# A decoder block on one core: VectorE instead of GpSimd makes the second MLP matrix's low halves, both token halves are streamed as one operand, and bias rows and sums of squares are rounded

## The reference, cut to what matters

```
h = rmsnorm(x, norm_attn);  proj = h @ w_in            # 512 tokens x 1024
o_nsa = nsa_attention(...)                             # T5 relative bias by distance
o_sb  = stick_breaking_attention(...)
mixed = sigmoid(..) * (o_nsa @ w_up_nsa) + sigmoid(..) * (o_sb @ w_up_sb)
x = x + mixed @ w_out
h = rmsnorm(x, norm_mlp)
x = x + square(relu(h @ w_ff1)) @ w_ff2                # 1024 -> 4096 -> 1024
return rmsnorm(x, norm_final)
```

## Time and profile before

| | |
|---|---|
| runs, us | 784.09, 781.94, 784.12 (median 784.09) |
| profiled execution, its own time | 782.67 us |
| its span from first to last instruction | 780.8 us |
| mean granted TensorE clock | 0.995 |
| busy share | PE 99%, PEld 83%, DVE 59%, ACT 50%, POOL 36% |

### The profile page before, as it was taken

How to read it: one execution, slowest core, us unless ns; L and a number is a source line. 1 busy time by engine, 2 the same in 40 slices (tenths; PEclk the granted TensorE clock), 3 DMA queues, 4 the chain that set the end, 5 groups by cost and what they waited for, 6 DMA issues and landing times.

```text
span 780.8 us, 11862 instructions
## 1 busy us (share of the span) xinstructions
PE 770.2 (99%) x4292; PEld 650.1 (83%) x4292; DVE 461.1 (59%) x936; ACT 387.9 (50%) x719; POOL 277.5 (36%) x366
## 2 busy tenths in 40 slices
PE   8999999999999999999999999999999999999996
PEld 6878888888877777778888888999999999999895
DVE  7446557787757676635544737556665556664334
ACT  6333314688966576574345644344444444443321
POOL 1255424511112332146455644333333322233640
PEclk9999999999999999999999999999999999999998
DMA  7954013210150110134232223332222333332213
GB/s 261 340 180 163 1 55 101 88 54 29 35 155 28 55 55 29 55 108 148 95 108 98 91 101 115 109 108 88 85 93 88 108 109 109 108 108 81 87 49 109
DMA packets 26006, 77.82 MB, mean 100 GB/s; under 512 B 3710, under 2 KB 6966, under 8 KB 25695
## 3 DMA queue, kind: packets, MB, share of 16 engines
q1 hardware_dynamic: 23868, 74.72, 29.0%
q10 hardware_dynamic: 2083, 2.37, 1.0%
HBM read 73.90 MB, written 2.13 MB: 97 GB/s over the span
## 4 chain that ended last, share of the span: by engine, by line
PE 93%; DVE 4%; ACT 2%; DMA 1%; issue 1%; DVEq 0%; ACTq 0%
PE bank L1508 31%; PE bank L1914 20%; PE bank L1888 5%; PE bank L1886 5%; PE bank L1884 5%; PE bank L1820 2%; PE bank L1802 2%; PE bank L1734 2%; PE bank L1859 2%; PE bank L1858 2%; PE bank L1854 2%; PE bank L1779 2%; PE bank L1752 1%; PE bank L1520 1%; PE bank L1521 1%; PE bank L1522 1%
## 5 line engine op out<-in xcount | busy, mean ns | idle before, releaser
L644 POOL TENSOR_TENSOR wlo<-wraw,whi 128x256 fp32r<-128x256 f32 x344 | 262.8, 796 | 461.4 <-ACT whi L685 378.6
L685 ACT ACTIVATE whi<-wraw 128x1024 fp32r<-128x1024 f32 x77 | 80.6, 1053 | 32.0 <-PE bank L1914 19.1
L1508 PE MATMUL bank<-hh,wlo 128*128 128x512 f32 x304 | 81.0, 396 | 0.7 <-DVE gm L1202 0.6
L1508 PE MATMUL bank<-hl,whi 128*128 128x512 f32 x304 | 80.6, 392 | 0.0
L1508 PE MATMUL bank<-hh,whi 128*128 128x512 f32 x304 | 79.6, 391 | 0.0
L1508 PEld LDWEIGHTS bank<-hh,whi 128*128 128x128 f32 x304 | 56.6, 188 | 11.7
L1508 PEld LDWEIGHTS bank<-hl,whi 128*128 128x128 f32 x304 | 56.4, 188 | 11.7 <-issue 0.2
L1508 PEld LDWEIGHTS bank<-hh,wlo 128*128 128x128 f32 x304 | 55.4, 188 | 12.8 <-DVE gm L1202 0.9
L1914 PE MATMUL bank<-r_l,whi 128*128 128x512 f32 x224 | 57.9, 390 | 0.0
L1914 PE MATMUL bank<-r_h,wlo 128*128 128x512 f32 x224 | 56.3, 392 | 0.0
L1914 PE MATMUL bank<-r_h,whi 128*128 128x512 f32 x224 | 55.7, 389 | 0.0
(11 more groups left out here) (310 smaller groups left out, 1647.1 us busy)
## 6 DMA issues: line engine op xcount, KB each, us to landing
wraw<-in_panels SPq DMA_DIRECT2D x101, 512.0 KB, 3.3
land<-in_panels SPq DMA_DIRECT2D x12, 512.0 KB, 4.5
w1k<-in_w SPq DMA_DIRECT2D x1, 2048.0 KB, 9.3
w1v<-in_w SPq DMA_DIRECT2D x1, 2048.0 KB, 14.8
svraw<-in_panels SPq DMA_DIRECT2D x4, 512.0 KB, 5.3
hank<-bias_by_distance SPq DMA_DIRECT2D x4, 512.0 KB, 6.3
x_res<-in_xT SPq DMA_DIRECT2D x4, 512.0 KB, 4.4
out_dram<-x_res SPq DMA_DIRECT2D x12, 128.0 KB, 1.8
```

What stands on the lines that cost most here:

```text
L644: ins = nc.gpsimd.tensor_tensor(wlo[:, s, k:k + 2], wraw[s][:, k:k + 2], whi[:, s, k:k + 2].bitcast(F32), ALU.subtract)
L685: A(whi[:, s], wraw[s][:], ACT.Copy).then_inc(w_hi, 1)
L1508: ins = M(b[:, cols], lhs, (xl if a == 1 else xh)[:, row + k, cols], start=(m == 0), stop=(m == 23))
```

## The change

1. `products` takes the input's high and low halves as one operand of two runs of 256 columns. For each of four weight tiles there is one matmul of 512 columns, high weights by (high, low), whose two results lie beside each other in a bank, and one of 256 columns, low weights by high input. That makes 8 matmuls in place of 12. `h2h` and `h2l` become halves of `h2`, `th` and `tl` of `tt`.
2. The right half of each bank now holds a part of the sum, so it is added by VectorE: two adds more in `c11`, one each in `c22`, `c12` and `c21`, and two new steps `m7_low` and `u2`. `c12` now starts with a ScalarE copy. TensorE waits for `u2_made` (VectorE) instead of `u2_copied` (ScalarE).
3. In the rounds, VectorE makes the low halves of the second matrix's panels (`second_matrix_low`, one instruction of 128x1024); GpSimd makes those of the first two and the last eight.
4. The four full-precision matmuls become pairs of rounded ones: the table, the two sums of squares and the ones are rounded into `relx_r`, `oneh_r`, `sqs_r`, `x_ss_r` and `ones_r`, with the low half as a second part.

```diff
@@ gpsimd
-            for p in range(P_SQK + RING * rounds, N_PLAIN):
-                low(p)
+            for m in range(2):
+                low(P_FF2 + m)
+            pool.wait_ge(w_lo, P_FF2 + 2 * N_SEVEN)
+            for m in range(2 * N_SEVEN, 32):
+                low(P_FF2 + m)
@@ scalar
+            act.wait_ge(sqs_done, KT)
+            A(sqs_r[:, 0], sqs[:], ACT.Copy).then_inc(sqs_hi, 1)
+            act.wait_ge(table_in, 16 * 3)
+            A(oneh_r[:], oneh[:], ACT.Copy).then_inc(table_hi, 1)
...
+            act.wait_ge(x_ss, KT)
+            A(x_ss_r[:, 0], mx[0][:], ACT.Copy).then_inc(x_ss_hi, 1)
...
+            def c12_high(j):
+                A(tmp[:, 0, T // 2:T], result(act, ("wa", j))[:, 0:T // 2], ACT.Copy).then_inc(c12_copied, 1)
...
-                    stored(act, ("wa", j - 1))
+                    c12_high(j - 1)
+                    act.wait_ge(pos1, j)
                     hidden_high(8 + 2 * j - 2)
@@ vector
+            dve.wait_ge(sqs_hi, 1)
+            V.tensor_tensor(sqs_r[:, 1], sqs[:], sqs_r[:, 0].bitcast(F32), ALU.subtract).then_inc(sqs_lo, 1)
...
+            dve.wait_ge(x_ss_hi, 1)
+            V.tensor_tensor(x_ss_r[:, 1], mx[0][:], x_ss_r[:, 0].bitcast(F32), ALU.subtract).then_inc(x_ss_lo, 1)
...
+            def second_matrix_low(m):
+                dve.wait_ge(w_lo, p)
+                dve.wait_ge(w_hi, p + 1)
+                V.tensor_tensor(wlo[:, s], wraw[s][:], whi[:, s].bitcast(F32), ALU.subtract).then_inc(w_lo, 1)
...
             def c11(j):
-                V.tensor_tensor(tmp[:, 0, near], bank[j % 2][:, near], tmp[:, 0, near], ALU.add).then_inc(c11_made, 1)
+                emptied(V.tensor_tensor(t, x[:, far], t, ALU.add), ("wx", j))
+                V.tensor_tensor(t, a[:, near], t, ALU.add).then_inc(c11_made, 1)
+                V.tensor_tensor(t, a[:, far], t, ALU.add).then_inc(c11_made, 1)
...
+            def u2(j):
+                dve.wait_ge(u2_copied, j + 1)
+                V.tensor_tensor(u2s[:], bank[j % 2][:, far], u2s[:], ALU.add).then_inc(u2_made, 1)
...
                 pair_second_low(j)
+                if j:
+                    second_matrix_low(2 * j + 1)
                 c11(j)
+                m7_low(j)
...
                     first_sums(j + 1)
+                u2(j)
+                if j + 1 < N_SEVEN:
                     third_sum(j + 1)
                     pair_first_low(j + 1, 0)
+                    second_matrix_low(2 * j + 2)
@@ tensor
-                filled(M(b[0:H, :], relx[:], oneh[:, T * i:T * i + T], start=True, stop=True), f"vec{i}")
+                for part in (1, 0):
+                    ins = M(b[0:H, :], relx_r[:, part], oneh_r[:, T * i:T * i + T], start=(part == 1), stop=(part == 0))
...
                 for k in range(4):
-                    M(o, wl[:, k], xh[:, k], start=(start and k == 0), stop=False, skip_group_check=True)
+                    M(o[:], wh[:, k], x[:, :, k], start=(start and k == 0), stop=False, skip_group_check=True)
                 for k in range(4):
-                    M(o, wh[:, k], xl[:, k], start=False, stop=False, skip_group_check=True)
-                for k in range(4):
-                    ins = M(o, wh[:, k], xh[:, k], start=False, stop=(stop and k == 3), skip_group_check=True)
+                    ins = M(o[:, 0:T // 2], wl[:, k], x[:, 0, k], start=False, stop=(stop and k == 3), skip_group_check=True)
...
-                pe_.wait_ge(u2_copied, j + 1)
+                pe_.wait_ge(u2_made, j + 1)
```

More of the change, by code:

```diff
@@ L329, in block_kernel @@
         dts = place("dts", [55, H, P], at=at_sbq + 6144)
+        relx_r = place("relx_r", [BUCKETS + 1, 2, H], F32R, at=at_sbq + 14080)
+        oneh_r = place("oneh_r", [BUCKETS + 1, 2 * T], F32R, at=tmp_at)
+        sqs_r = place("sqs_r", [P, 2, T], F32R, at=at_sbq)
         relx = place("relx", [BUCKETS + 1, H], at=at_sbq + 10240)
@@ L342, in block_kernel @@
         svraw = [place(f"svraw{c}", [P, 8, P], at=at_g + 4096 * c) for c in range(RING)]
+        ones_r = place("ones_r", [P, P], F32R)
         kd1 = place("kd1", [P, 2, T], F32R, at=tmp_at)
@@ L983, in _ @@
             V.memset(relx[BUCKETS:BUCKETS + 1, :], BIG).then_inc(set_done, 1)
+            dve.wait_ge(set_done, 1)
+            V.tensor_copy(ones_r[:], ones[:]).then_inc(set_done, 1)
             for g in range(G):
@@ L1388, in pair_second_low @@
                 V.tensor_tensor(wlo[:, 3, 4:8], land[:, 4:8], whi[:, 3, 4:8].bitcast(F32), ALU.subtract).then_inc(pd_lo, 1)
+            def second_matrix_low(m):
+                p = P_FF2 + m
+                s = slot(p)
+                dve.wait_ge(w_lo, p)
+                dve.wait_ge(w_hi, p + 1)
+                V.tensor_tensor(wlo[:, s], wraw[s][:], whi[:, s].bitcast(F32), ALU.subtract).then_inc(w_lo, 1)
             def c11(j):
+                a, x, t = bank[j % 2], bank[2], tmp[:, 0, near]
+                dve.wait_ge(x_copied, j + 1)
+                emptied(V.tensor_tensor(t, x[:, far], t, ALU.add), ("wx", j))
@@ L1397, in c22, with m7_low @@
+                positive(t, t, near)
+            def m7_low(j):
+                t = tmp[:, 1, far]
+                dve.wait_ge(m7_copied, j + 1)
+                V.tensor_tensor(t, bank[3][:, far], t, ALU.add).then_inc(c22_made, 1)
+            def u2(j):
+                dve.wait_ge(u2_copied, j + 1)
+                V.tensor_tensor(u2s[:], bank[j % 2][:, far], u2s[:], ALU.add).then_inc(u2_made, 1)
             def c22(j):
+                a, t = bank[j % 2], tmp[:, 1, far]
                 dve.wait_ge(v_ready, j + 1)
-                dve.wait_ge(m7_copied, j + 1)
@@ L1401, in c22 @@
-                V.tensor_tensor(tmp[:, 1, far], bank[j % 2][:, near], tmp[:, 1, far], ALU.add).then_inc(c22_made, 1)
+                dve.wait_ge(c22_made, 3 * j + 1)
+                V.tensor_tensor(t, a[:, near], t, ALU.add).then_inc(c22_made, 1)
+                dve.wait_ge(c22_made, 3 * j + 2)
+                V.tensor_tensor(t, a[:, far], t, ALU.add).then_inc(c22_made, 1)
             def c12(j):
-                a = result(dve, ("wa", j))
-                emptied(positive(tmp[:, 0, far], a[:, near], far), ("wa", j))
@@ L1407, in c21 @@
-            def c21(j):
-                r = result(dve, ("wr", j))
-                dve.wait_ge(u2_copied, j + 1)
-                emptied(V.tensor_tensor(tmp[:, 1, near], r[:, near], u2s[:], ALU.add), ("wr", j))
+                t = tmp[:, 0, far]
+                dve.wait_ge(c12_copied, j + 1)
+                emptied(V.tensor_tensor(t, bank[j % 2][:, far], t, ALU.add), ("wa", j))
+                stored(dve, ("wa", j))
+                positive(t, t, far).then_inc(pos1, 1)
+            def c21(j):
+                r, t = result(dve, ("wr", j)), tmp[:, 1, near]
+                dve.wait_ge(u2_made, j + 1)
+                V.tensor_tensor(t, r[:, near], u2s[:], ALU.add).then_inc(c21_made, 1)
+                dve.wait_ge(c21_made, j + 1)
+                emptied(V.tensor_tensor(t, r[:, far], t, ALU.add), ("wr", j))
@@ L1612, in _ @@
             b = claim(pe_, "rms")
-            pe_.wait_ge(set_done, 4)
-            pe_.wait_ge(sqs_done, KT)
-            filled(M(b[:], ones[:], sqs[:], start=True, stop=True), "rms")
+            pe_.wait_ge(set_done, 5)
+            pe_.wait_ge(sqs_lo, 1)
+            for part in (1, 0):
+                ins = M(b[:], ones_r[:], sqs_r[:, part], start=(part == 1), stop=(part == 0))
+            filled(ins, "rms")
             bias_rows(0)
@@ L1875, in _, with products @@
             b = claim(pe_, "rms2")
-            pe_.wait_ge(x_ss, KT)
-            filled(M(b[:], ones[:], mx[0][:], start=True, stop=True), "rms2")
+            pe_.wait_ge(x_ss_lo, 1)
+            for part in (1, 0):
+                ins = M(b[:], ones_r[:], x_ss_r[:, part], start=(part == 1), stop=(part == 0))
+            filled(ins, "rms2")
             for n in range(2, 8):
                 panel(P_FF + n, ("ff", 0, n), h2h, h2l)
-            def products(o, wh, wl, xh, xl, start, stop):
+            def products(o, wh, wl, x, start, stop):
                 for k in range(4):
-                    M(o, wl[:, k], xh[:, k], start=(start and k == 0), stop=False, skip_group_check=True)
+                    M(o[:], wh[:, k], x[:, :, k], start=(start and k == 0), stop=False, skip_group_check=True)
                 for k in range(4):
-                    M(o, wh[:, k], xl[:, k], start=False, stop=False, skip_group_check=True)
-                for k in range(4):
-                    ins = M(o, wh[:, k], xh[:, k], start=False, stop=(stop and k == 3), skip_group_check=True)
+                    ins = M(o[:, 0:T // 2], wl[:, k], x[:, 0, k], start=False, stop=(stop and k == 3), skip_group_check=True)
                 return ins
@@ L1929, in _ @@
-                r = claim(pe_, ("wr", j))[:, near]
+                filled(products(x, whi[:, 2, 4:8], wlo[:, 2, 4:8], h2[:, :, 4:8, near], True, True), ("wx", j))
+                r = claim(pe_, ("wr", j))
```

(4 more changed lines are left out.)

52 lines of the change are left out of this document (31 added, 21 removed).

## The result

The changed kernel takes 777.44 us (median of five executions, 776.99 to 778.6). The kernel before takes 782.36 (median of five, 781.27 to 784.12). The ratio is 0.9933, with a 95% interval from 0.9916 to 0.995: faster by 0.7%, against about 0.3% that a measurement of this kernel can tell. The forecast was 777.2, in a range from 775.2 to 781.8.

What follows compares the result with a forecast made beforehand. The prediction took TensorE's issued matmuls to bound the kernel, since it never waits in a round. From 782.67 us it took 3.5 for joined products and 2.0 for rounded pairs, giving 777.2 us, range 775.2 to 781.8.

Steps and rivals of the forecast that it cites:

- What bounds the kernel: MLP rounds: TensorE is busy for all of 21.02 us, so what it has to issue counts.
- Part 1: Seven products a round with 8 matmuls in place of 12: 0.29 us less a round, 3.5 us in all.
- Rival 1: Joined matmuls in the products: two runs cost what two matmuls cost, 1.0 us lost, total 781.7; chance 0.12.
- the smaller saving: Joined products: with the skill's 2.5 ns fixed per matmul, only 0.8 us gained before width changes, total about 780 to 781.
- Part 2: Seven more VectorE adds a round, 2.9 us, all beside TensorE's work: 0 us; tightest room 1.5 us at `u2`.
- What a miss would cost: VectorE's adds in the rounds: once the room is gone, each microsecond late costs one a round, 12 in all.
- Part 3: Low halves of the second matrix moved to VectorE, 2.4 us a round in its idle time: 0 us.
- Part 4: Four full-precision matmuls (`rms`, two bias rows, `rms2`), 3.77 us, become rounded pairs of 1.81 us: 2.0 us gained.
- Rival 3: Near the start: the attention stage's chains set the pace, 1.4 us of gain lost, total 778.6; chance 0.08.
- The sum: Whole kernel: 782.67 of the profiled execution less 3.5 and 2.0 gives 777.2 us; from the runs' median 778.6.

Runs made afterwards that it cites:

- split kernel: The changed kernel with every 512-column matmul of the seven products cut into two of 256 columns: 781.47 us, ratio 0.9983.
- three delays: The changed kernel with three extra VectorE instructions a round, unread and each waiting for the last, ahead of `u2`: 786.95 us (one execution).
- four delays: The changed kernel with four extra VectorE instructions a round, unread and each waiting for the last, ahead of `u2`: 793.88 us, ratio 1.0155.

## Why the prediction came out as it did

**What bounds the kernel**: right. TensorE was busy in all of a round before and is so after; the round fell by what it issues less.

**Part 1** (3.5 us): right, in sign and size. (What is streamed as one operand are the high and the low half of the same 256 tokens, not the two token halves that the title names.) A round is 20.71 us, 20.73 was forecast; 12 x 0.31 = 3.7. The price that no row of before showed, a 512-column matmul that streams two separate runs, is 0.90 / 4 = 0.225 to 0.227 us, the value taken. The split kernel returned the rounds to 21.02, so no other part of the change takes a share in it. Rival 1 fell, and so did the smaller saving that follows from the fixed part of 2.5 ns which the Trainium skill states ("TensorE: Matmul & The Clock Gate", section "Back-to-back issue gap"): by that figure, an estimate, 0.8 us at most, measured 3.7. The prediction took this figure for a rule against the part, but the section gives it for a matmul by itself; for a stream of weight loads and matmuls it gives about 131 ns at 512 columns. This case's rows agree with neither: 227 ns at 512.

**Part 2** (0 us): right. The rooms forecast and found: `u2` 1.5 and 1.47 us, `c22` 1.65 and 1.67, bank 3 1.7 and 1.7 (`c21`'s second add ends at 517.17, the next product into bank 3 starts at 518.90; the prediction's own times, 497.1 and 498.94, give 1.8). `c11` was expected to be made at 502.9; its last add ends at 502.08 (501.66 + 0.42), nearly 3 us ahead of the product at 505.06, in a round whose full product starts 0.79 us earlier than in before (499.59 against 500.38), so the forecast was met. Walking VectorE's queue instruction by instruction was enough; no price had to be guessed.

**What a miss would cost** (each microsecond late costs a microsecond a round): the price is right, the room was read too wide. `u2` 0.73 us later still, from three delays to four, is 0.73 us more in a round. But the rounds grow from 1.30 us of lateness on and not from 1.47: the signal takes 0.05 (555.25 to 555.30), and the matmuls behind a stop take 0.12 more. The forecast for the change did not use this. The expectations for three and four delays forecast waits of 0.5 and 1.2 us, and the profile printed just these, yet the rounds grew by 0.75 and 1.48: the step that failed there is to take the wait for the growth of the round. Their own numbers, 2.15 - 1.47 and 2.9 - 1.47, come nearer with 0.7 and 1.4.

**Part 3** (0 us): right in the time, 17.3 us of VectorE a round against 17.6 forecast. The term missed GpSimd's silence, which gives some of VectorE's instructions their time back: `positive` of 512 columns takes 1.25 us in before (496.72) and 0.69 in after (517.21). The reader should note that this part, a visible share of the change, brings nothing: with it undone the rounds keep 20.71.

**Part 4** (2.0 us): right mechanism, the term too large. The instructions took 3.77 us, the pairs take 0.56 + 0.55 + 0.55 + 0.45 = 2.11 and not 1.81: a gain of **1.66**, and the kernel with the old form confirms 1.6. At `rms2`, between wide matmuls, the pair takes the two pitches that were assumed; at the three places ahead of 280-column matmuls it takes 0.1 us more. What that tenth is was not taken apart. What feeds the pairs was in time, as worked out, if a little closer at `rms2`: the remainder for it ends at 437.7, 436.8 was forecast, 441.60 wants it.

**Rival 3** fell. The attention stage did not give the early gain back: from its first long product to the end of that stage before passes in 350.31 us (36.48 to 386.79), after in 350.26 (36.61 to 386.87), and the 1.2 us won ahead of it stay won (23.61 to 36.48 is 12.87 us in before, 24.93 to 36.61 is 11.68 in after).

**The sum** said 5.5 us, the traces from landmark to end say 5.3, the medians 4.9 and 5.5. That it is so near is in part luck: part 1 was taken 0.1 to 0.2 too small and part 4 0.3 too large, which cancels for the most part. The sum was made against one execution (782.67), and the profiled one of after took 778.6, not 777.2: 1.3 us of that is the later start, where TensorE's clock rose later; no step of the prediction could give it, and its range held it. From the median of before's five executions (782.36) the same sum gives 776.9, so the 0.2 us between 777.2 and the measured median says less than it seems.

## What to carry to other kernels

Where TensorE is busy without a gap, count its instructions and not only its columns: each rounded matmul of this kernel has 13 ns beyond its columns, so two that share a weight tile and stream different operands can be one, if one access reaches both and their results may stand side by side in a bank. Before giving the extra adds to another engine, walk its queue to each place where TensorE needs it; the rooms read so were right to 0.05 us for the two tightest places. Count such a room to the weight load ahead of the matmul, and a stop as more than the wait the profile prints. And compare executions from a landmark behind the first loads when the change is smaller than the scatter of the start.

## What the runs showed that I had not expected

- A stop of TensorE costs more than its recorded wait: 0.47 us on record is 0.75 of round, 1.2 is 1.48. The four matmuls behind the stop take 1.03 us and not 0.91, and the recorded end of a wide matmul lies 0.16 us behind the point where the next could start.
- 2.4 us of new work on VectorE a round cost it 1.4: with GpSimd idle the low halves of the weight panels take 692 ns on average, 904 beside it.
- The first 15 us vary by up to 2.6 us between the executions profiled (landmark from 14.01 to 16.61; 2.0 between two of the same code), and the landmark comes late where TensorE's clock rises late. What is behind it repeated to 0.1 us in the three with the same rounds and pairs (760.4 each).
